# Router logits of seven tiles: weights stationary on column halves of the TensorE array, joined and turned by one product

## The reference

```
h = layer_norm(DEEPNORM_ALPHA * h + mlstm_mixer(h), ln1_g, ln1_b)
grp_logits = xf @ w_group + b_group                 # (T, 4)
g_top = argmax(grp_logits)
exp_logits = (xf @ w_router + b_router)             # (T, 4 groups, 8)
top_vals, top_idx = top_k(exp_logits[g_top], 2)
# each (token, expert) pair gets a slot in its expert's list;
# out = layer_norm(DEEPNORM_ALPHA * h + weighted sum of the two experts' outputs)
```

## Time and profile before

| | us |
|---|---|
| median of 3 runs | 1124.29 |
| lowest and highest run | 1123.3, 1124.64 |
| the profiled execution | 1124.6 |
| its span, first to last instruction | 1122.8 |
| router stage, 396.7 to 483.2 in the profile | 86.5 |
| of it, PE busy | 83.66 |

### The profile page before, as it was taken

How to read it: one execution, slowest core, us unless ns; L and a number is a source line. 1 busy time by engine, 2 the same in 40 slices (tenths; PEclk the granted TensorE clock), 3 DMA queues, 4 the chain that set the end, 5 groups by cost and what they waited for, 6 DMA issues and landing times.

```text
span 1122.8 us, 15319 instructions
## 1 busy us (share of the span) xinstructions
PE 1093.7 (97%) x5369; PEld 899.2 (80%) x5369; DVE 799.9 (71%) x1127; ACT 626.4 (56%) x698; POOL 216.0 (19%) x188
## 2 busy tenths in 40 slices
PE   8999999999999999979999999999999999999986
PEld 7778899788888787858888888888888888888852
DVE  4220422144557787679999999998989989898787
ACT  5312222224335310147887878778788888888644
POOL 4000112000000000020434323143332423323110
PEclk9999999999999999999999999999999999999998
DMA  8612314802123222159999999999999999999885
GB/s 304 224 50 101 122 43 129 276 20 75 39 77 114 113 76 94 54 203 381 398 380 367 397 375 390 391 380 394 378 380 383 385 389 370 391 392 379 312 328 217
DMA packets 69273, 288.32 MB, mean 257 GB/s; under 512 B 16229, under 2 KB 20453, under 8 KB 43620
## 3 DMA queue, kind: packets, MB, share of 16 engines
q1 hardware_dynamic: 56224, 258.34, 60.7%
q0 software_dynamic: 11840, 25.09, 6.1%
q10 hardware_dynamic: 1156, 4.20, 1.0%
HBM read 266.66 MB, written 37.75 MB: 271 GB/s over the span
## 4 chain that ended last, share of the span: by engine, by line
PE 93%; DVE 3%; DMA 2%; issue 1%; ACT 0%; DVEq 0%; POOL 0%; POOLq 0%; ACTq 0%
PE bank L1645 26%; PE bank L1647 26%; PE bank L1646 26%; PE bank L1994 3%; PE bank L2094 1%; PE bank L2029 1%; PE bank L1832 1%; PE bank L1834 1%; PE bank L1881 1%; PE bank L1837 1%; DMA expert_rows<-yt,dix 1%; PE bank L1846 1%; PE bank L1790 1%; PE bank L1873 1%; DMA xg<-h_rows,tokrow 1%
## 5 line engine op out<-in xcount | busy, mean ns | idle before, releaser
L1645 PE MATMUL bank<-whi,xghi 128*128 128x512 f32 x512 | 203.5, 397 | 0.6 <-DVE xglo L1489 0.6
L1647 PE MATMUL bank<-whi,xglo 128*128 128x512 f32 x512 | 200.6, 392 | 0.0
L1646 PE MATMUL bank<-wlo,xghi 128*128 128x512 f32 x512 | 200.2, 391 | 0.0
L1476 DVE TENSOR_TENSOR wlo<-raw_down,whi 128x2048 fp32r<-128x2048 f32 x64 | 146.3, 2291 | 28.0 <-ACT whi L819 27.9
L1645 PE MATMUL bank<-whi,xhi 128*128 128x512 f32 x384 | 156.2, 407 | 0.9 <-ACT num L762 0.6
L1647 PE MATMUL bank<-whi,xlo 128*128 128x512 f32 x384 | 151.7, 395 | 0.0
L1646 PE MATMUL bank<-wlo,xhi 128*128 128x512 f32 x384 | 151.7, 395 | 0.0
L1476 DVE TENSOR_TENSOR wlo<-raw,whi 128x2048 fp32r<-128x2048 f32 x64 | 146.3, 2288 | 4.5 <-ACT whi L819 3.6
L1476 DVE TENSOR_TENSOR wlo<-raw_up,whi 128x2048 fp32r<-128x2048 f32 x64 | 146.2, 2285 | 0.0
L819 ACT ACTIVATE whi<-raw_up 128x2048 fp32r<-128x2048 f32 x64 | 122.4, 1915 | 25.8 <-PE bank L1647 25.4
L819 ACT ACTIVATE whi<-raw_down 128x2048 fp32r<-128x2048 f32 x64 | 122.4, 1912 | 23.7 <-PE bank L1647 23.7
(11 more groups left out here) (342 smaller groups left out, 1715.7 us busy)
## 6 DMA issues: line engine op xcount, KB each, us to landing
raw<-l_w_gate SPq DMA_DIRECT2D x64, 1024.0 KB, 8.3
raw_up<-l_w_up SPq DMA_DIRECT2D x64, 1024.0 KB, 8.4
raw_down<-l_w_down SPq DMA_DIRECT2D x64, 1024.0 KB, 8.6
raw<-l_w_in SPq DMA_DIRECT2D x5, 2048.0 KB, 10.0
yy<-expert_rows SPq DMA_DIRECT2D x8, 1024.0 KB, 7.9
xt<-x_cols SPq DMA_DIRECT2D x8, 512.0 KB, 4.9
o_rows<-stage POOLq DMA_DIRECT2D x16, 256.0 KB, 2.9
qkT<-qk_rows SPq DMA_DIRECT2D x16, 256.0 KB, 3.8
```

The source lines that it names most:

```text
L1476: tt(wlo[k][:, halves(p)], raw_e[k][:, halves(p)], whi[k][:, halves(p)].bitcast(F32), ALU.subtract).then_inc(e_lo[k], 1)
L1645: t.matmul(out, lh, rh, start=first, stop=False)
L1646: t.matmul(out, lh, rl, start=False, stop=False)
L1647: return t.matmul(out, ll, rh, start=False, stop=last)
```

## The change

For tiles 0 to 6 `logits(i)` has its operands exchanged. The weights `wgr` (128x40) are stationary and the 128 columns of `h1T` move, so the result comes out as 40 logits x 128 tokens. Even chunks go to rows 0 to 39 of bank 2, columns 256 to 383, and odd chunks to rows 64 to 103; by the output's first row a product sits on the lower or the upper 64 columns of the array. Each half accumulates four chunks. ACT copies both halves to a tile `lgT` whose other rows are zero (`logit_parts`), and one new product, `fold_logits(i)`, with `lgT` stationary and a 0/1 matrix `fold` moving, adds the halves and turns them to 128 tokens x 40, where `choice` reads them as before. Tile 7 keeps the old form (`logits_by_token`). POOL fills `lgT` and `fold` once. Pieces of `out_half` are cut differently to make room for the fold.

```
+    lgT = over("wg16", "lgT", [P, P])
+    fold = over("wg_raw", "fold", [P, NL])
+    PART_COLS = slice(256, 256 + P)
 POOL:
+        g.memset(lgT[:], 0.0)
+        g.memset(fold[:], 0.0)
+        pool.drain()
+        for rows in (0, HALF_ROWS):
+            g.affine_select(out=fold[:], in_=fold[:], compare_op=ALU.not_equal, fill=1.0, base=-rows, pattern=[[-1, NL]], channel_multiplier=1)
+            pool.drain()
 ACT:
         def z_T(i):
-                wait(act, N["lg_mm"], i)
+                wait(act, N["lgT_mm"], i)
+        def logit_parts(i):
+            act.wait_ge(N["lgT_mm"], i + 1)
+            wait(act, N["lg_mm"], i)
+            if i == 0:
+                act.wait_ge(N["ones_ready"], 1)
+            a.activation(lgT[0:NL], ps[F_BANK[0]][0:NL, PART_COLS], ACT.Copy)
+            a.activation(lgT[HALF_ROWS:HALF_ROWS + NL], ps[F_BANK[0]][HALF_ROWS:HALF_ROWS + NL, PART_COLS], ACT.Copy).then_inc(N["lgT_cp"], 1)
         for i in range(NT - 1):
             z_T(i)
+            logit_parts(i)
             h1_store(i)
 PE:
             for k in range(KC):
+                rows = slice(HALF_ROWS * (k % 2), HALF_ROWS * (k % 2) + NL)
+                last = t.matmul(ps[F_BANK[0]][rows, PART_COLS], wgr[:, k, :], h1T[:, k, :], start=k < 2, stop=k >= KC - 2)
+            last.then_inc(N["lgT_mm"], 1)
+        def fold_logits(i):
+            pe.wait_ge(N["lgT_cp"], i + 1)
+            t.matmul(ps[F_BANK[0]][:, 0:NL], lgT[:], fold[:], start=True, stop=True).then_inc(N["lg_mm"], 1)
 PE, tile 0 (the piece before z_T(1)):
-        out_half(2, 1, range(4, KC))
+        out_half(2, 1, range(4, 6))
+        fold_logits(0)
+        out_half(2, 1, range(6, KC))
 PE, the loop for tiles 4 to 6:
-            out_half(i, 1, range(0, 4))
+            out_half(i, 1, range(0, 2))
+            fold_logits(i - 1)
+            out_half(i, 1, range(2, 5))
             ranks(i - 1)
-            out_half(i, 1, range(4, KC))
+            out_half(i, 1, range(5, KC))
```

More of the change, by code:

```diff
@@ L48 @@
 NL = GPAD + NE
+HALF_ROWS = 64
 def wait(eng, sem, value):
@@ L318, in build @@
         v_mm v_cp ones_ready kx_mm ks_done ksm_done e_mm ew_done s_mm sw_done b_row_mm qs_done n_mm num_done
-        u_mm c_done rs_done nn_done gated_done ot_mm o_hi o_lo y_mm z_done h1_done h1_scale h1_mm ht_mm ht_cp lg_mm lg_done
+        u_mm c_done rs_done nn_done gated_done ot_mm o_hi o_lo y_mm z_done h1_done h1_scale h1_mm ht_mm ht_cp lgT_mm lgT_cp lg_mm lg_done
         cc_mm cc_cp cc_out cc_in wg_scaled r_hot rk_mm r_slot list_mm counted cnt_mm routed routed_n
@@ L1880, in logits, with logits_by_token @@
             for k in range(KC):
+                rows = slice(HALF_ROWS * (k % 2), HALF_ROWS * (k % 2) + NL)
+                last = t.matmul(ps[F_BANK[0]][rows, PART_COLS], wgr[:, k, :], h1T[:, k, :], start=k < 2, stop=k >= KC - 2)
+            last.then_inc(N["lgT_mm"], 1)
+        def logits_by_token(i):
+            pe.wait_ge(N["ht_cp"], 2 * i + 2)
+            wait(pe, N["r_slot"], i)
+            for k in range(KC):
                 last = t.matmul(ps[F_BANK[0]][:, 0:NL], h1T[:, k, :], wgr[:, k, :], start=k == 0, stop=k == KC - 1)
             last.then_inc(N["lg_mm"], 1)
+        def fold_logits(i):
+            pe.wait_ge(N["lgT_cp"], i + 1)
+            t.matmul(ps[F_BANK[0]][:, 0:NL], lgT[:], fold[:], start=True, stop=True).then_inc(N["lg_mm"], 1)
         def ranks(i):
@@ L1947, in _ @@
         z_T(2)
-        out_half(3, 1, range(0, 4))
+        out_half(3, 1, range(0, 2))
+        fold_logits(1)
+        out_half(3, 1, range(2, 5))
         ranks(1)
         token_list(0)
-        out_half(3, 1, range(4, KC))
+        out_half(3, 1, range(5, KC))
         out_half(4, 0, range(0, 2))
@@ L1955, in _ @@
         z_T(3)
-        out_half(4, 0, range(2, 5))
+        out_half(4, 0, range(2, 4))
+        fold_logits(2)
+        out_half(4, 0, range(4, 6))
         ranks(2)
-        out_half(4, 0, range(5, KC))
+        out_half(4, 0, range(6, KC))
         token_list(2)
         logits(3)
-        out_half(4, 1, range(0, 4))
+        out_half(4, 1, range(0, 2))
+        fold_logits(3)
+        out_half(4, 1, range(2, 5))
         ranks(3)
-        out_half(4, 1, range(4, KC))
+        out_half(4, 1, range(5, KC))
         for i in range(5, NT):
@@ L1976, in _ @@
         awake(Z_BANK[0], 2)
-        logits(NT - 1)
+        logits_by_token(NT - 1)
         for q in range(2):
```

## The result

The changed kernel takes **1127.54 us** (median of 7 runs, 1125.76 to 1128.97), the kernel before 1124.29 (7 runs, 1123.3 to 1125.23). The ratio is 1.0026, 95% interval 1.0015 to 1.0037: slower, by 3.25 us in the medians. The forecast was 1127.5 in a range of 1126.0 to 1131.7.

A forecast was written before the change was run, and what follows sets the result against it. PE, 97% busy, was taken as the bound, its list threaded through a DVE chain. Delays of 2.56 at tile 2 and 0.6 at tiles 4 to 6, 3.2 on 1124.6, less 0.3 to the median: 1127.5 us, range 1126.0 to 1131.7.

The forecast's parts named there:

- The overlap: Sixteen part records on PE: the column halves work at once, about 0.055 apart, holding PE 0.92 us instead of 1.7.
- the first rival: Parts on PE: halves don't overlap, records hold PE 1.7 us; run +7.1, 1131.4 us; chance 0.14.
- the pitch follows the moving columns: Argument from PE's rows: a record's spacing depends on moving columns, not on array columns in use (4 or 128).
- The block: Parts of each tile on PE: 0.92 us for the records plus 0.09 for the next product's slower first step.
- entering a narrow form costs nothing: PE's change from 128-column to 32-column product: no extra time, the ordinary 0.23 step, read at 211.12.
- The drain rival: PE's array runs empty at each change of form: 0.33 more per block; run +4.8, 1129.1 us; chance 0.08.
- The fold: New product on PE per tile: two records 0.21 plus 0.09 on the next product, 0.30 us.
- Tile 2: DVE reads logits at 426.05 instead of 423.49, behind `z_T(3)` and two chunks; `z_T(4)` moves by all 2.56 us.
- Tiles 4 to 6: PE idles about 0.9 us before ranks, three chunks not covering the choice; 0.2 more per tile, 0.6 for three.
- The tail: Tile 7 and the experts behind it: untouched, so the router stage's delay reaches the end whole.
- a sign of being wrong: Experts' stretch: the prediction is wrong if this stretch changes by itself.
- POOL: Two fills, two selects and drains take some 1.3 us before its last fill; SP's following work is due 30 us later.

The follow-up runs named there:

- e4: Changed kernel with three unused full-width bf16 products put among the parts of each tile; 1129.71 us (one run).
- second traces: Changed kernel and kernel before, both unedited, each traced once more; these executions took 1128.26 and 1125.1 us.
- e2: Changed kernel with two output chunks and the fold of tile 2 moved ahead of `z_T(3)`; 1125.22 us, ratio to before 1.0007.
- e3: Changed kernel with the ranks of tiles 4 to 6 one output chunk later; 1124.81 us, ratio to before 0.9998.
- e6: Kernel before, without the split, with the ranks of tiles 4 to 6 one output chunk later; 1123.09 us, ratio 0.9989.
- e7: Changed kernel with folds of tiles 1 and 2 ahead of the next transpose and ranks of tiles 4 to 6 one chunk later; 1121.71 us, ratio 0.9975.
- e8: Changed kernel with the split kept only at tiles 4 to 6, ranks one chunk later there; 1120.89 us, ratio to before 0.9967.
- e1: Changed kernel with the parts grouped, four even chunks then four odd, instead of alternating; 1127.8 us, ratio to before 1.0033.
- e10: Split at tiles 4 to 6 only, ranks later, plus DVE's second expert-weight subtraction held until POOL's first gather and drain; 1124.83 us, ratio 1.0001.
- e9: Kernel before with DVE's second expert-weight subtraction held until POOL issued the first gather, with a drain; 1129.07 us, ratio 1.0040.

## Why the prediction was right

The direction and the mechanism held, and the undisturbed loss in the stretch was 3.91 for a predicted 3.2. The steps:

- **The overlap.** Predicted: about 0.055 a record, 0.92 in all, and held four times as likely as none. Measured 0.053, or 0.85 in all, the floor that the prediction named. Right, and the first rival is out. One sentence behind it goes too far: that the pitch follows the moving columns. By its own rows 40 moving columns take 0.107 a record and 128 take 0.11, so the 40 are no cheaper; the sum used only that.
- **The block.** Predicted 0.92 + 0.09 = 1.01, measured 1.20. The step that failed is "entering a narrow form costs nothing". It was read from one place, where the products of 512 columns on both sides show no gap, and was carried to float32 parts, where e4 shows 0.24 in and out. The drain rival had the right mechanism at 0.33, and 0.08 was too small a chance for it.
- **The fold.** Predicted 0.30, measured 0.23. Block and fold: 1.43 against 1.31, so PE saves 0.36 a tile and not 0.48.
- **Tile 2.** Predicted: DVE reads 2.56 late, for `z_T(3)` and two chunks ahead of the fold, and the whole of it reaches `z_T(4)`. Measured 2.94 late at the reading and 2.96 at `z_T(4)` (second traces). The mechanism was right, and e2 took 1.82 of it out. The 0.4 is in the main the block's 0.2, at tiles 0 and 1. PE's wait at `z_T(3)` was to be 1.1 and was 0.90.
- **Tiles 4 to 6.** Predicted 0.2 each with 0.9 of waiting before ranks; measured 0.32 each with 0.76, 1.09 and 0.77. e3 shows that these waits can be worked in, e6 that part of them was there before the change. The 0.1 is the block again: the fold starts 2.51 behind the parts instead of 2.39.
- **The clock** was not in the sum. It cost 0.76 in one of two traces of the changed kernel.
- **The tail** was called untouched and was not; the prediction had named that as a sign of being wrong. The experts' own 549.9 us are unchanged, but from `z_T(7)` to the first hidden_T the changed kernel gives back 0.46 in the second pair and 3.94 in the first. The median came out at 3.25 and not at 3.9: that fits a tail that is often better after the change, but two traces of each don't measure how often.
- **POOL.** The fills and selects were put at 1.3 us before the last fill; it starts at 208.37 instead of 201.74, 6.6 later, of which 0.7 was there ahead of the new instructions; the first select alone lasts 1.90 after 3.16 of idle time. Harmless, since SP's piece due at 232.37 starts at 231.56 all the same: the cover named in the prediction was wide enough for a term more than four times too small. ACT's two copies, 0.27 each, fit beside the chunks.

So the agreement to 0.1 us in the median is in part luck: a stretch that cost 0.7 more and a tail that gave some back.

## What to carry to other kernels

A faster product in two steps pays only if the second step stands where the reader of the result was served before; here the saving of 0.36 a tile was real, and the place of the folds of tiles 1 and 2, behind a transpose and two chunks, cost nearly all of the 2.9 that `z_T(4)` came late (0.2 are left in e7). First find who reads the result and how early, then move the fold, then count the product's own time. And before crediting a new form with a gain, try the new order on the old form: later ranks without any split (e6) gave more in tiles 4 to 6 than with it, by the one trace of each. The medians of e7 and e8 lie below that of e6 even so, and nothing here explains that; whether the split can pay with a fold that comes earlier in tiles 4 to 6 is open.

## What the runs showed of the hardware

- Two float32 products of 128 moving columns on separate column halves overlap fully when they come in turn: 0.053 a record, where one half alone has 0.11 (e1) and the old form 0.107. Grouped by half, the sixteen overlap in part (0.085).
- A change between full-width products and the parts costs 0.24 there and back (e4), of which 0.09 on the way in stands behind bf16 products too. From the 128-column product of 512 moving columns to the 32-column one no gap shows.
- A gather on POOL that starts beside DVE's subtraction of two SBUF tensors ends 0.96 or 0.97 us after the end of the last subtraction that had started before it. In the traces that is 1.09 or up to 3.24 us for the same instruction. The Trainium skill ("SBUF — State Buffer", SBUF: two separate sides) tells of an exclusive lock on a port pair between a DVE operation with two SBUF inputs and a GpSimd operation that reads SBUF; these traces agree with it in that the gather waits for the whole subtraction, but they don't show the port.
- A drain on POOL behind an indirect DMA held what came behind it for 4.2 and 6.0 us past the end of the gather's instruction (e10, e9).
- With waits of 2.06 to 2.22 us at one place TensorE's clock fell to its lower level for 3.4 us in some executions and stayed up in others, of one kernel too (2.06 with a fall, 2.09 without, in the two traces of after).
